# Loading the gate and up matrices of a mixture of experts as 4 MB transfers, with all of gate ahead of up, in an fp32 encoder block

## What is computed

```python
def expert_choice_swiglu(h, w_router, w_gate, w_up, w_down):
    cap = EC_CAPACITY_FACTOR * seq // N_EXPERTS                     # 64
    aff = jax.nn.softmax(jnp.einsum('bsd,de->bse', h, w_router).astype(jnp.float32), axis=-1)
    g, idx = lax.top_k(jnp.swapaxes(aff, 1, 2), cap)
    xin = jax.vmap(lambda hb, ib: hb[ib])(h, idx)
    a = jnp.einsum('becd,edf->becf', xin, w_gate)
    u = jnp.einsum('becd,edf->becf', xin, w_up)
    y = jnp.einsum('becf,efd->becd', jax.nn.silu(a) * u, w_down) * g[..., None].astype(h.dtype)
    return jax.vmap(lambda ib, yb: jnp.zeros((seq, dm), yb.dtype).at[ib.reshape(-1)].add(yb.reshape(-1, dm)))(idx, y)
```

## Time and profile before

| | |
|---|---|
| median of 3 runs | 888.64 us (886.47 to 889.47) |
| the profiled execution | 886.65 us, its span 884.6 us |
| TensorE (matmul) busy | 855.1 us, 97% of the span |
| loads of weights, first and last part of the experts' stage | 430.5 to 870.5 us |
| HBM read | 235.92 MB (10^6), 269 GB/s over the span |

### The profile page before, as it was taken

How to read it: one execution, slowest core, us unless ns; L and a number is a source line. 1 busy time by engine, 2 the same in 40 slices (tenths; PEclk the granted TensorE clock), 3 DMA queues, 4 the chain that set the end, 5 groups by cost and what they waited for, 6 DMA issues and landing times.

```text
span 884.6 us, 10960 instructions
## 1 busy us (share of the span) xinstructions
PE 855.1 (97%) x4475; PEld 532.1 (60%) x4475; DVE 358.2 (40%) x639; ACT 269.1 (30%) x476; POOL 25.7 (3%) x51
## 2 busy tenths in 40 slices
PE   9999999999999999999999999999998988989995
PEld 8999877587878888888534443343433433334332
DVE  5468778586606345326412213232221311312404
ACT  6333767675634233217101010010100101001203
POOL 1040000000000000001000000000000000000001
PEclk9999999999999999999999999999999999999998
DMA  9523213023133424853999999999999999999993
GB/s 256 122 75 96 72 36 100 9 66 90 43 119 110 112 79 140 310 220 133 360 413 425 422 429 427 426 428 427 427 430 426 426 427 430 427 429 427 427 420 153
DMA packets 80373, 238.73 MB, mean 270 GB/s; under 512 B 8002, under 2 KB 63426, under 8 KB 65604
## 3 DMA queue, kind: packets, MB, share of 16 engines
q1 hardware_dynamic: 75040, 235.94, 67.5%
q10 hardware_dynamic: 5284, 2.09, 0.9%
HBM read 235.92 MB, written 2.10 MB: 269 GB/s over the span
## 4 chain that ended last, share of the span: by engine, by line
PE 82%; DMA 11%; DVE 3%; ACT 1%; issue 1%; POOL 0%; DVEq 0%; ACTq 0%; SPq 0%; POOLq 0%
PE psum L1497 18%; PE psum L1529 12%; DMA wslot<-in_w_down 11%; PE psum L1025 11%; PE psum L1027 10%; PE psum L1026 10%; PE psum L1457 3%; PE psum L1548 3%; PE psum L1215 2%; PE psum L1227 2%; PE psum L1185 1%; PE psum L1201 1%; PE psum L1509 1%; PE psum L1465 1%; PE psum L1237 1%
## 5 line engine op out<-in xcount | busy, mean ns | idle before, releaser
L1497 PE MATMUL psum<-wslot,xinT 128*64 128x512 f32 x1016 | 226.5, 595 | 6.6 <-DMA wslot<-in_w_up 2.7
L1497 PEld LDWEIGHTS psum<-wslot,xinT 128*64 128x64 f32 x1016 | 70.5, 137 | 146.7 <-issue 135.4
L1529 PE MATMUL psum<-wslot,actT 128*64 128x512 f32 x504 | 114.1, 597 | 7.5 <-DMA wslot<-in_w_down 7.5
L1025 PE MATMUL psum<-hT_hi,w_hi 128*128 128x512 f32 x224 | 89.1, 398 | 0.0
L1026 PE MATMUL psum<-hT_lo,w_hi 128*128 128x512 f32 x224 | 87.6, 391 | 0.0
L1027 PE MATMUL psum<-hT_hi,w_lo 128*128 128x512 f32 x224 | 87.5, 391 | 0.0
L1701 DVE TENSOR_TENSOR w_lo<-w_raw,w_hi 128x1024 fp32r<-128x1024 f32 (+1 forms) x52 | 60.1, 1180 | 63.8 <-ACT w_hi L682 63.5
L1529 PEld LDWEIGHTS psum<-wslot,actT 128*64 128x64 f32 x504 | 34.6, 136 | 75.3 <-issue 68.5
L965 ACT ACTIVATE actT<-psum 128x512 f32<-128x512 f32 x16 | 9.6, 597 | 184.4 <-PE psum L1509 184.4
L2077 DVE TENSOR_TENSOR x<-x,psum 128x512 f32<-128x512 f32 x56 | 34.7, 681 | 74.4 <-PE psum L1548 74.4
L2069 DVE TENSOR_TENSOR y_lo<-psum,y_hi 64x512 fp32r<-64x512 f32 x32 | 22.0, 689 | 101.9 <-ACT y_hi L975 101.4
(11 more groups left out here) (259 smaller groups left out, 1239.6 us busy)
## 6 DMA issues: line engine op xcount, KB each, us to landing
wslot<-in_w_gate SPq DMA_DIRECT2D x27, 2048.0 KB, 29.0
wslot<-in_w_up SPq DMA_DIRECT2D x27, 2048.0 KB, 29.6
wslot<-in_w_down SPq DMA_DIRECT2D x24, 2048.0 KB, 28.0
w_raw<-in_w_in SPq DMA_DIRECT2D x40, 512.0 KB, 4.6
wslot<-in_w_down SPq DMA_DIRECT2D x15, 1024.0 KB, 31.2
wslot<-in_w_gate SPq DMA_DIRECT2D x10, 1024.0 KB, 10.2
wslot<-in_w_up SPq DMA_DIRECT2D x9, 1024.0 KB, 10.6
w_raw<-in_w_out SPq DMA_DIRECT2D x8, 512.0 KB, 4.8
```

The costliest lines, as they stand in the source:

```text
L1025: pe.matmul(out_, s_hi, m_hi, start=(k == 0), stop=False)
L1497: mm = pe.matmul(bank[2 * e + n][CAP * f:CAP * f + CAP, :], xinT[:, HALF * h + k, CAP * e:CAP * e + CAP], wslot[place_of(m)][:, k % PART, ...
L1529: mm = pe.matmul(bank[4 + e][CAP * f:CAP * f + CAP, :], actT[:, e, k, CAP * h:CAP * h + CAP], wslot[place_of(m)][:, k % PART, SEQ * f:SEQ ...
```

## The change

Gate and up of the pairs 1 to 6 are loaded whole, 4 MB in one transfer, where both halves are not yet past (from half 14, which is `up` of expert 0 of pair 1, to the end of pair 6: 3 + 5 x 4 = 23 transfers in the place of 46). A partition then gets eight adjacent rows of the matrix, 32 KB in a row. The four places of such a transfer have to be neighbours, so the homes are laid out as four `double_slot`s. From pair 1 on the order is gate h0, gate h1, up h0, up h1 of each expert (`BY_MATRIX`), for the loads and for TensorE; pair 0 keeps the old order. Half h of gate or up is now the second or first four of a partition's eight rows, in the pairs 0 and 7 as well ("(p h k) n"), and the tokens are read with a step of 8 elements to match. Down and the parted halves keep their size. The early loads are in another order, since other parts live in the homes that come free first.

```diff
-    wide_slot = [sb(f"wslot{i}", [HALF * D], kib) for i, kib in
-                 enumerate((W0 + 32, 0, 16, W0 + 48, 32, 64, W0 + 64, W0 + 80))]
+    double_slot = [sb(f"wslot{i}", [KC * D], kib) for i, kib in enumerate((0, W0 + 64, 32, W0 + 32))]
+    wide_slot = [double_slot[(i - 1) % 8 // 2][:, HALF * D * (i % 2 == 0):][:, 0:HALF * D] for i in range(8)]
...
+        BY_MATRIX = [(w, h, e) for e in range(2) for w in (w_gate, w_up) for h in range(2)] + HALVES[8:]
...
+        def halves_of(p):
+            return BY_MATRIX if p else HALVES
+        def first_of_transfer(m):
+            half = m // 2
+            if parted(half):
+                return m
+            return 4 * (half // 2) if doubled(half) else 2 * half
+        def doubled(half):
+            return half % len(HALVES) < 8 and FIRST_PARTED.stop <= half < (PAIRS - 1) * len(HALVES)
...
-            if m % 2 and not parted(m // 2):
+            if first_of_transfer(m) != m:
                 return
...
-                matrix, h, e = HALVES[entry]
-                return matrix[0, 2 * p + e].rearrange("(h p k) n -> h p (k n)", h=2, p=P)[h]
+                matrix, h, e = halves_of(p)[entry]
+                order = "(h p k) n -> h p (k n)" if matrix is w_down else "(p h k) n -> h p (k n)"
+                return matrix[0, 2 * p + e].rearrange(order, h=2, p=P)[h]
...
+                if doubled(half):
+                    if half % 2:
+                        return
+                    for m in range(2 * half, 2 * half + 4):
+                        wait_place_free(sp, m)
+                    p, entry = divmod(half, len(HALVES))
+                    matrix, _, e = halves_of(p)[entry]
+                    place = place_of(2 * half)
+                    sp.dma_start(double_slot[place // 4][:, :],
+                                 matrix[0, 2 * p + e].rearrange("(p k) n -> p (k n)", p=P)).then_inc(w_slot_in[place], 16)
+                    return
...
-            load_part(6)
-            load_part(8)
+            load_first(0, 1)
...
-                                x2[:, c, :].rearrange("p (h i k) -> p h k i", h=2, k=HALF), ACT.Copy,
+                                x2[:, c, :].rearrange("p (i h k) -> p h k i", h=2, k=HALF), ACT.Copy,
...
-                for h in range(2):
-                    if p or h:
-                        pe.wait_ge(xin_done, xin_count(p, h))
...
-                    for n, w in enumerate((w_gate, w_up)):
-                        for k in range(HALF):
+                steps = [(n, h, k) for n in range(2) for h in range(2) for k in range(HALF)]
+                if p == 0:
+                    steps.sort(key=lambda step: step[1])
+                for step, (n, h, k) in enumerate(steps):
```

More of the change, by code:

```diff
@@ L174, in encoder_block @@
     PART = HALF // 2
-    wide_slot = [sb(f"wslot{i}", [HALF * D], kib) for i, kib in
-                 enumerate((W0 + 32, 0, 16, W0 + 48, 32, 64, W0 + 64, W0 + 80))]
+    double_slot = [sb(f"wslot{i}", [KC * D], kib) for i, kib in enumerate((0, W0 + 64, 32, W0 + 32))]
+    wide_slot = [double_slot[(i - 1) % 8 // 2][:, HALF * D * (i % 2 == 0):][:, 0:HALF * D] for i in range(8)]
     wslot = [wide[:, PART * D * i:PART * D * (i + 1)].rearrange("p (k n) -> p k n", n=D)
              for wide in wide_slot for i in range(2)]
-    wslot += [sb(f"wslot_once{i}", [PART, D], 48 + 8 * i) for i in range(2)]
+    wslot += [sb(f"wslot_once{i}", [PART, D], 64 + 8 * i) for i in range(2)]
     xn_hi = sb("xn_hi", [NT, D], W0, F32R)
@@ L183, in encoder_block @@
     xn_raw = [sb(f"xn_raw{i}", [SEQ], kib) for i, kib in enumerate((107.5, 96))]
[L184 to L187, removed]
+    y_hi = sb("y_hi", [D], 64, F32R)
+    y_lo = sb("y_lo", [D], 68, F32R)
+    give = sb("give", [2, SEQ], 72, F32R)
+    actT = sb("actT", [2, NT, P], 76)
     xinT = sb("xinT", [KC, 2 * CAP], 96)
@@ L199, in encoder_block @@
     fin = sb("fin", [NT, D], W0)
-    junk = sb("junk", [2, SEQ], 60)
+    junk = sb("junk", [2, SEQ], 76)
     g2 = small[:, 8:16]
@@ L389, in encoder_block @@
         HALVES += [(w_down, h, e) for e in range(2) for h in range(2)]
+        BY_MATRIX = [(w, h, e) for e in range(2) for w in (w_gate, w_up) for h in range(2)] + HALVES[8:]
         PAIRS = NE // 2
         def part_at(p, matrix, h, e, k):
-            return 2 * (len(HALVES) * p + HALVES.index((matrix, h, e))) + k // PART
+            return 2 * (len(HALVES) * p + halves_of(p).index((matrix, h, e))) + k // PART
+        def halves_of(p):
[7 more added lines that the diff above has]
+            return half % len(HALVES) < 8 and FIRST_PARTED.stop <= half < (PAIRS - 1) * len(HALVES)
         def parted(half):
@@ L419, in wait_part_in @@
         def wait_part_in(eng, m):
-            if m % 2 and not parted(m // 2):
+            if first_of_transfer(m) != m:
                 return
-            own = [n for n in tenants[place_of(m)] if n <= m and (n % 2 == 0 or parted(n // 2))]
+            own = [n for n in tenants[place_of(m)] if n <= m and first_of_transfer(n) == n]
             eng.wait_ge(w_slot_in[place_of(m)], 16 * len(own))
@@ L549, in load_half, with load_first @@
                 sp.dma_start(wide_slot[place // 2][:, :], rows_of(half)).then_inc(w_slot_in[place], 16)
+            def load_first(*places):
+                for i in places:
+                    load_part(tenants[i][0])
             load_x(0)
@@ L559, in _ @@
                     sp.wait_ge(pv_done, OA + OB)
-                    load_half(0)
+                    load_first(14, 15)
                 if strips[n] == ("out", D // P - 1):
@@ L567, in _ @@
                     sp.wait_ge(proj_done, g_at[("gate", KC - 1, 1)] + 1)
-                    load_half(1)
-            load_half(2)
+                    load_first(2, 3)
+            load_first(4, 5)
             sp.wait_ge(m_lo_done, KC)
-            load_part(6)
-            load_part(8)
+            load_first(0, 1)
             wait_split(sp, len(strips) - 1)
-            load_part(9)
-            load_part(10)
+            load_first(10, 11)
             sp.wait_ge(proj_done, len(groups))
-            for m in (7, 11, 12, 13, 14, 15, 16, 17):
-                load_part(m)
+            load_first(6, SLOTS + 1, 7, 8, 9, 12, 13, SLOTS)
             for half in range(9, len(HALVES) * PAIRS):
@@ L701, in _ @@
                                allow_slow_non_contiguous=True).then_inc(gains_in, 16)
-            act_.dma_start(g2_rows, norm2_g[0].rearrange("(h p k) -> p h k", h=2, p=P),
+            act_.dma_start(g2_rows, norm2_g[0].rearrange("(p h k) -> p h k", h=2, p=P),
                            allow_slow_non_contiguous=True).then_inc(gains_in, 16)
@@ L934, in _ @@
                 act_.activation(xn_raw[n % 2][:, :].rearrange("p (k i) -> p k i", k=HALF),
-                                x2[:, c, cols].rearrange("p (i k) -> p k i", k=HALF), ACT.Copy,
+                                x2[:, c, :].rearrange("p (i h k) -> p h k i", h=2, k=HALF)[:, h], ACT.Copy,
                                 scale=rstd[:, c:c + 1]).then_inc(xn_copied, 1)
@@ L1476, in gate_up @@
             def gate_up(p, e, between):
-                for h in range(2):
-                    if p or h:
+                steps = [(n, h, k) for n in range(2) for h in range(2) for k in range(HALF)]
+                if p == 0:
+                    steps.sort(key=lambda step: step[1])
+                for step, (n, h, k) in enumerate(steps):
+                    m = part_at(p, (w_gate, w_up)[n], h, e, k)
+                    if k == 0 and (p or h):
                         pe.wait_ge(xin_done, xin_count(p, h))
-                    if h == 0 and p == PAIRS - 1 and e:
+                    if step == 0 and p == PAIRS - 1 and e:
                         pe.wait_ge(gf_done, 2)
-                    if h == 0 and p:
+                    if step == 0 and p:
                         pe.wait_ge(actT_done, 2 * p - 1 + e)
@@ L1488, in gate_up @@
                             pe.wait_ge(give_done, p + 1)
-                    for n, w in enumerate((w_gate, w_up)):
-                        for k in range(HALF):
[L1491 to L1503, removed]
+                    if k % PART == 0:
+                        wait_part_in(pe, m)
+                    if m < 2 and k % PART == 0:
+                        pe.wait_ge(xin_done, m + 1)
+                    for f in range(2):
+                        mm = pe.matmul(bank[2 * e + n][CAP * f:CAP * f + CAP, :],
+                                       xinT[:, HALF * h + k, CAP * e:CAP * e + CAP],
+                                       wslot[place_of(m)][:, k % PART, SEQ * f:SEQ * f + SEQ],
+                                       start=(h == 0 and k == 0), stop=(h == 1 and k == HALF - 1))
+                    if k % PART == PART - 1:
+                        mm.then_inc(w_slot_used[place_of(m)], 1)
+                    between(step)
             def turn_act(i):
@@ L1935, in low_xn @@
```

(3 more changed lines are left out.)

## The result

The change is slower by about 0.4%: 891.18 us median (889.98 to 893.63, 9 runs) against 887.85 for the kernel before in the same comparison; the ratio is 1.0046, interval 1.0036 to 1.0056. So 3 to 4 us, where the forecast had 2.5 and gave "within 0.3%" the largest chance (0.46).

A forecast was written before the change was run, and what follows sets the result against it. Stream and TensorE were taken to end together, so the stream's delivery counts: gaps 3.4 us less 1.3 saved make the stream 2.2 later, plus 0.3 for TensorE, from 887.6 to 890.1 us (+2.5), range 886.8 to 893.8.

The forecast's parts named there:

- The bound: Tail of the kernel: stream and TensorE end together, the last part used 0.2 us after it landed.
- The saving of 0.055 us per transfer: Full stream: a 4 MB transfer takes 9.735 us against 9.79 for two of 2 MB; 23 save 1.3 us.
- rival 2: The 23 large transfers: 32 KB rows run 1.6% slower, +7.4 us in all, 895.0; chance 0.18.
- rival 1: The 32 KB rows move in 16 KB packets, so nothing is saved: +3.7 us, 891.3; chance 0.15.
- the 20 later transfers give back 1.1: Stream after C: 3.3 us late there, it regains 1.1 us and ends 2.2 us later.
- The gaps: Stream in pair 1: it runs empty before A for 0.9 us and before C for 2.5, together 3.4 us.
- A: First 4 MB transfer of pair 1: issued at 462.39, after 0.9 us of nothing, landing at 474.7.
- C: Up of expert 1 of pair 1: issued at 484.39, after 2.5 us of nothing, landing at 496.7.
- B: 4 MB transfer of pair 1 between A and C: issued in time at 470.98, no gap, landing at 484.5.
- What TensorE adds: Pair 6, expert 1: TensorE waits for 4 MB where it began on the first 2, 0.3 us more.
- Rival 4: The 23 transfers fewer: a rule of 2 us per transfer would take off 46 us, 842; chance 0.01.
- Rival 3: Whole stream: larger transfers lose fixed cost and small setbacks, gaps a third of those counted: -4 us, 883.6; chance 0.14.

The follow-up runs named there:

- e3: The changed kernel with only the three transfers of pair 1 in 4 MB, the other 20 in halves again: 891.08 us, ratio 1.0038 to the kernel before.
- e4: The changed kernel with only the 16 transfers of pairs 2 to 5 in 4 MB, pairs 1 and 6 in halves: ratio 0.9994 to the kernel before.
- e1: The changed kernel with every gate and up half again loaded as 2 MB, order and layout kept: 887.73 us, ratio 1.0001 to the kernel before.
- e2: The changed kernel with up of expert 1 of pair 1 alone split into two of 2 MB: 889.48 us, ratio 1.0018 to the kernel before.
- e7: The changed kernel with pairs 1 to 5 in 4 MB and pair 6 in halves: ratio 1.0041 to the kernel before.
- e8: The changed kernel with pairs 2 to 6 in 4 MB and pair 1 in halves, no transposes: ratio 1.0002 to the kernel before.
- e11: The changed kernel with only pair 6 in 4 MB, plus eight transposes before the wait for its gate of expert 1: ratio 1.0008 to the kernel before.
- e10: The changed kernel with only pair 6 in 4 MB, four transfers, no transposes: ratio 1.0010 to the kernel before.
- e5: The changed kernel plus eight transposes on TensorE before its wait for gate of expert 1 in pairs 4, 5 and 6: ratio 1.0041 to the kernel before.

## Why the prediction came out as it did

**The bound** was read rightly. Stream and TensorE end together before; a gap early in the stream is paid at the end 380 us later (e3: 3.3 us in the stream, 3.4 in the time). The prediction also said that a shorter stream helps only where TensorE is let go earlier at 799.18, and that is what e4 shows.

**The saving of 0.055 us per transfer** was right in kind and a little low: 9.72 us per 4 MB, not 9.735, against 9.79. Rows of 32 KB run no slower (rival 2 falls) and the saving is there (rival 1 falls). In the profiles all of it reaches the end: e4, with 16 transfers and no gap, ends 1.2 us ahead of e1, from the first use on. In the times it is 0.6 us (e4 less e1), with an interval that holds both 0 and 1.2, so that it stays open whether the term "the 20 later transfers give back 1.1" is too large for the time.

**The gaps** were priced at 0.9, 0 and 2.5, 3.4 us together. A landed 0.6 late, against 9.72 after the landing ahead of it. C started 2.3 us after its issue, not 2.6. And B, which was issued in time, landed 1.2 us late by its slowest engine (the fifteenth of the 16 was done at 486.6, the last at 487.6), which shortened the gap before C to 1.2: 0.6 + 1.2 + 1.2 = 3.0 us in the change's trace, and 3.2 in e3's. A fourth piece was not foreseen: behind C all 16 engines end within 0.3 us of each other, and at the second half of down after it one falls back again, done at 509.8 where the fifteenth was at 508.3, 1.5 us. This stands in all five traces in which C is one transfer (1.1 to 1.6 us) and not in e2's (0.2). Against it, the setbacks beyond 511 us are fewer, 1.7 us in all in the change's trace and 2.5 in that of before. So the sum held and its parts did not, which is luck in part. Why one engine falls back there stays open. In time, pair 1 in 4 MB costs 3.3 us (e3 less e1, 0.37%), 4.2 (e7 less e4, 0.47%) and 2.8 to 3.9 (the change less e8).

**The term that was mis-sized is "What TensorE adds", 0.3 us.** It took TensorE as free exactly when up lands, and at full speed. It measured 2.1 us in both profiles of the change: from the landing of the second half of down to the end of its work TensorE took 5.8 us, where the kernel before took 3.7 and the prediction had 4.0. With the clock held the prediction's picture is right: in e11 up lands at 791.6 and its first record runs at 791.7. In the change up lands at 793.8 and its first record runs at 795.5. What was left out is the 2.5 us of idle ahead of gate of expert 1, which the sum had seen ("7.2 us of work fit into the 9.7 until the next") and called free: it was not, since the clock fell behind it and 28 records took 1.5 to 1.7 us longer. With the clock held 0.6 us is left, not 0.3: up begins 0.1 us after its landing, and its 32 records take 7.09 us, not 6.87. Over all executions the wait costs less than in the profiled ones, 0.9 us in e10.

**The sum.** Predicted: 3.4 - 1.3 + 0.3 = +2.4, rounded to +2.5. Now, from the time of e3, e4 less e1 and e10: 3.4 - 0.6 + 0.9 = +3.7, between the two measurements, 4.1 and 3.0; each of the three is known to about 1 us, so that this agreement proves little. The profiles, from the first use on, put it otherwise: +2.4 in the stream up to the landing that sets the end, where 2.2 was forecast, and +2.1 in TensorE, where 0.3 was. Either way "just inside no change" was missed, and the late wait that TensorE pays is part of it. The median of 891.18 is 1.1 above the number given.

Rival 4 falls too: 23 transfers fewer did not take 2 us each off, as 9.72 us per 4 MB against 9.79 per two of 2 MB shows. The Trainium skill ("DMA: Bandwidth & Descriptors", Latency and other measured facts) reports copies slowed by large power-of-two pitches from 512 KiB up; at the 32 KiB of this kernel nothing of the kind shows, since 4 MB flow at 431 GB/s (4,194,304 bytes in 9.72 us). Rival 3 (faster) had the small setbacks of the slowest engine go with fewer transfers. They did not go: of the 11.2 us between two landings at 724.1 and 735.3 in the change's trace, 1.5 are such a setback.

## What to carry to other kernels

A larger transfer is issued when its last piece of room is free, so it trades stock for size: where the transfers on their way at that moment last less than the 2.3 to 2.6 us from issue to flow, the stream runs dry, and those are the transfers to split (e8, with pair 1 in halves, is at the time of the kernel before). In a full queue the size from 2 to 4 MB is worth 0.07 us per transfer, which is little even 23 times. Where the stream sets the pace, a coarser wait is not free for the engine behind it: its idle comes in one piece, and if its clock falls there, near the end, nothing catches it up (2.1 us in the profiles of the change, 0.9 us, 0.0 to 1.8, in the times of e10).

## What the runs showed of the hardware

- **Idle and TensorE's clock.** The thirteen traces have some fifty idles of TensorE on loads between 1.1 and 1.6 us in the experts, and the granted clock stayed at 1.00 after each. Of thirteen idles of 1.9 to 2.0 us one went with the lower level (764.0 in e5), of 21 of 2.5 to 2.9 us twelve did. At gate of expert 1 of pair 6 it fell behind every idle of 2.6 us: five profiles of five. Each fall in the experts lasted 3.4 us. Why some long idles went without one stays open.
- **The start.** The first four matmuls of the gains take 1.98 us in six profiles, 2.3 in two (e2, e5) and 3.78 in five; with 3.78 all that follows is some 2 us later. The runs of the change fall in two groups, 889.98 to 891.18 and 893.22 to 893.63; that the start separates them was not shown, since only profiled executions have a trace.
- **Issue to flow.** C, a 4 MB transfer issued 1.1 us ahead of the landing of all that was on its way, lands 12.0 us after its issue, 2.3 us above the 9.72 in a full stream; 1 MB into an empty queue lands after 5.1 us, 2.6 above its 2.48.
- **The slowest engine.** In a full stream the 16 DMA engines end one transfer up to 3.5 us apart in the trace of the change, and the last sets the landing. Behind the gap ahead of C they end 0.3 us apart.
